# The last sequence's values in one half chunk, and the sample's output projection and MLP among the prompt's last MLP chunk

## The reference, cut to what matters

```python
def layer_out(x, attn, pool, mods, w_out, norm_mlp, w_up, w_down):
    _, _, g1, sh2, sc2, g2 = mods
    x = x + g1 * (jnp.concatenate([attn, pool], axis=-1) @ w_out)      # w_out 1024 x 1024
    h = rms_norm(x, norm_mlp) * (1 + sc2) + sh2
    return x + g2 * (jnp.square(jax.nn.relu(h @ w_up)) @ w_down)       # 1024 x 4096, 4096 x 1024

def reference(...):
    # prompt
    attn = moba_prompt(q, k, v, rel_bias)
    xp = layer_out(xp, attn, pool, mods, w_out, norm_mlp, w_up, w_down)
    # sample: scores over all past blocks, the best 3 blocks and the own one are weighed
    attn = moba_sample(q, k, v, cache_k, cache_v, l, page_table, rel_bias)
    xs = layer_out(xs, attn, pool, mods, w_out, norm_mlp, w_up, w_down)
    return rms_norm(xp, norm_final), rms_norm(xs, norm_final), ...
```

## Time and profile before

| what | us |
|---|---|
| timed runs | 897.68 median (897.31 to 902.81, 3 runs) |
| profiled launch | 903.88 |
| its span, first to last instruction | 902.0 |
| TensorE busy in the span | 841.3 (93%), 7634 matmuls |
| VectorE, ScalarE, GpSimd busy | 441.7, 338.1, 293.3 |
| mean granted TensorE clock | 0.976 |
| moved by DMA | 254.02 MB, mean 282 GB/s |

### The profile page before, as it was taken

The page is one execution under the profiler, slowest core; times in us unless marked ns, Lnnn a source line. Parts: engine busy times, 40 slices in busy tenths (PEclk is TensorE's granted clock), DMA queues, the critical chain, the costliest instruction groups (busy, mean ns, idle before and its releaser), DMA issues.

```text
span 902.0 us, 20195 instructions
## 1 busy us (share of the span) xinstructions
PE 841.3 (93%) x7634; PEld 592.8 (66%) x7634; DVE 441.7 (49%) x845; ACT 338.1 (37%) x701; POOL 293.3 (33%) x191
## 2 busy tenths in 40 slices
PE   5899999998999699999999999999999999999664
PEld 4577776666766266666666666666766666677553
DVE  2643222774776965575574564565564332013211
ACT  4133223886124646145145145154154254331110
POOL 0330003956221634244243343343333344440000
PEclk9699999999999699999999999999999999999988
DMA  9942236694999879999999999999999797779995
GB/s 294 326 153 94 94 106 256 194 343 147 323 299 308 284 260 333 303 310 333 304 301 341 300 322 322 298 314 329 301 318 373 247 333 257 235 251 349 399 397 213
DMA packets 167825, 254.02 MB, mean 282 GB/s; under 512 B 10454, under 2 KB 69419, under 8 KB 167755
## 3 DMA queue, kind: packets, MB, share of 16 engines
q1 hardware_dynamic: 166995, 250.66, 81.9%
q0 software_dynamic: 768, 2.51, 0.7%
HBM read 248.56 MB, written 4.75 MB: 281 GB/s over the span
## 4 chain that ended last, share of the span: by engine, by line
PE 82%; DVE 6%; DMA 3%; issue 3%; ACT 3%; SPq 3%; POOL 0%; DVEq 0%; ACTq 0%
PE PS L1523 78%; DMA W<-in_cache_v_dram 2%; SPq L501 2%; DMA mixT<-in_x_prompt_dram 1%; DVE W L1308 1%; DVE xT L1376 1%; PE PS L1872 1%; PE PS L1746 1%; PE PS L2055 1%; DVE mixT L1248 1%; DVE hT L1087 1%; SPq L496 1%; ACT mixT L878 1%; DVE mixT L1245 0%; DVE stat L1250 0%
## 5 line engine op out<-in xcount | busy, mean ns | idle before, releaser
L691 POOL TENSOR_TENSOR W_split<-W,W_split 128x1024 fp32r<-128x1024 f32 x72 | 172.8, 2399 | 289.0 <-ACT W_split L851 133.9
L1523 PE MATMUL PS<-gT_split,W_split 128*128 128x512 f32 x576 | 197.9, 404 | 1.2 <-DVE xT L1376 0.5
L1308 DVE STREAM_TRANSPOSE W<-rwT 128x512 f32<-128x512 f32 x256 | 162.7, 682 | 39.1 <-PE PS L1523 30.5
L1523 PE MATMUL PS<-rwT_split,W_split 128*128 128x512 f32 x512 | 174.9, 405 | 0.0
L1523 PE MATMUL PS<-hT_split,W_split 128*128 128x512 f32 x416 | 162.0, 399 | 0.5 <-ACT mixT L924 0.5
L1523 PEld LDWEIGHTS PS<-gT_split,W_split 128*128 128x128 f32 x576 | 108.1, 188 | 50.5 <-issue 14.8
L1523 PEld LDWEIGHTS PS<-rwT_split,W_split 128*128 128x128 f32 x512 | 97.1, 190 | 34.3 <-issue 14.8
L1523 PE MATMUL PS<-kT_split,W_split 128*128 128x512 f32 x256 | 100.0, 391 | 0.0
L851 ACT ACTIVATE W_split<-W 128x1024 fp32r<-128x1024 f32 x32 | 33.9, 1059 | 168.9 <-DMA W<-in_w_up_dram 168.8
L1376 DVE SCALAR_TENSOR_TENSOR xT<-PS,mods,xT 128x512 f32<-128x512 f32 x64 | 47.3, 742 | 97.0 <-PE PS L1523 96.8
L1523 PEld LDWEIGHTS PS<-hT_split,W_split 128*128 128x128 f32 x416 | 79.3, 191 | 16.7 <-issue 1.6
(11 more groups left out here) (276 smaller groups left out, 966.5 us busy)
## 6 DMA issues: line engine op xcount, KB each, us to landing
rwT<-in_cache_k_dram SPq DMA_DIRECT2D x256, 256.0 KB, 4.2
W<-in_cache_v_dram SPq DMA_DIRECT2D x256, 256.0 KB, 3.9
W<-in_w_ada_dram SPq DMA_DIRECT2D x12, 2048.0 KB, 10.8
W<-in_w_up_dram SPq DMA_DIRECT2D x32, 512.0 KB, 5.6
W<-in_w_down_dram SPq DMA_DIRECT2D x32, 512.0 KB, 5.5
W<-in_w_down_dram SPq DMA_DIRECT2D x5, 2048.0 KB, 17.3
W<-in_w_in_dram SPq DMA_DIRECT2D x3, 2048.0 KB, 7.9
rwT<-in_w_up_dram SPq DMA_DIRECT2D x3, 2048.0 KB, 11.4
```

The source lines that it names most:

```text
L691: pool.tensor_tensor(rows_part(RAW, q, W_split), rows_part(RAW, q), rows_part(HIGH, q, W_split), ALU.subtract).then_inc(w_low, 1)
L1308: dve.transpose(ktb[u % 2][:, :, g, :], k_ring[:, j % SLOTS, pg, :]).then_inc(kt_ev, 1)
L1523: return pe.matmul(out, lhsT, rhs, start=start, stop=stop, **kw)
```

## The change

The last sequence's values are weighed in `down(LAST - 1, ...)` alone, one unit after each tile. `turn_heads(LAST)`, the output projection, its fold, the mean square and the sample's MLP step 0 go among the matmuls of `up(LAST, ...)`; steps 1 to 4 go among those of `down(LAST, ...)`; steps 5 to 7 stay behind, now with the prompt's final rows (two blocks in step 5, one each in steps 6 and 7). The tail's slots are four instead of six, and SP's, ScalarE's and VectorE's lists follow the new order. Nothing is computed in another way.

```diff
-        tail_landed = [sem(f"tail_landed{i}") for i in range(6)]
+        tail_landed = [sem(f"tail_landed{i}") for i in range(4)]
...
-        tail_slots = [mixT[...], W[:, 0, :], rw[:, 0:4096], W[:, 1, :], hT[...], rw[:, 4096:8192]]
+        tail_slots = [mixT[...], W[:, 0, :], rw[:, 0:4096], W[:, 1, :]]
... SP
-            for u in range(UNITS):
-                section(LAST - 1, u, keys=False, values=u < UNITS - 1)
+            sp.wait_ge(up_ps, HP * LAST)
+            load_down(LAST - 1, 3)
+            for j in range(2, 4):
+                load_values(LAST, j)
+            for q in range(PARTS):
+                if q < PARTS - 1:
+                    for j in range(4 * q + 4, 4 * q + 8):
+                        load_values(LAST, j)
+                sp.wait_ge(dn_ps, FT * (LAST - 1) + 2 * q + 2)
+                load_up(LAST, q)
             sp.wait_ge(v_used, BLOCKS * DB)
             load_tail(3)
-            sp.wait_ge(up_ps, HP * DB)
-            load_down(LAST, 3)
+            sp.wait_ge(so_ps, 1)
             load_tail(4)
             load_tail(5)
-            sp.wait_ge(so_ps, 1)
+            sp.wait_ge(up_ps, HP * LAST + 1)
+            load_down(LAST, 0)
+            sp.wait_ge(up_ps, HP * LAST + 2)
+            load_down(LAST, 1)
+            sp.wait_ge(sup_ps, 1)
             load_tail(6)
+            sp.wait_ge(up_ps, HP * LAST + 3)
+            load_down(LAST, 2)
+            sp.wait_ge(sdn_ps, 1)
             load_tail(7)
+            sp.wait_ge(up_ps, HP * LAST + 4)
+            load_down(LAST, 3)
             for n in range(8, N_TAIL):
                 sp.wait_ge((sup_ps, sdn_ps)[n % 2], (n - TAIL_SLOTS) // 2)
                 load_tail(n)
... ScalarE, after front(LAST - 1); sample_relu(i) is the Relu of step i
+            up_high(LAST, 2)
+            up_high(LAST, 3)
+            hidden(LAST, 0)
+            act.wait_ge(so_ev, 1)
+            act.activation(hTs[:, :, :], xTs[:, :, :], ACT.Square).then_inc(sq_done, 1)
+            act.wait_ge(sms_ps, 1)
+            act.activation(rstds[:, :], bank(1, P, NS), ACT.Sqrt, ...).then_inc(root_done, 1)
+            hidden(LAST, 1)
+            down_high(LAST, 0)
+            sample_relu(0)
+            hidden(LAST, 2)
+            down_high(LAST, 1)
+            hidden(LAST, 3)
+            down_high(LAST, 2)
+            down_high(LAST, 3)
+            for i in range(1, N_CH):
+                sample_relu(i)
+                if i == 5:
+                    final_norm(0)
+                    final_norm(1)
+                elif i > 5:
+                    final_norm(i - 4)
             final_norm(TT)
... VectorE, in the loop over the steps; the rest of the sample's norm stands ahead of it
                 dve.wait_ge(sup_ps, i + 1)
                 dve.tensor_copy(up_sums, bank(0, P, P)).then_inc(sup_copied, 1)
+                if i == 1:
+                    ... square of step 1
+                    down_out(LAST, 0)
+                    down_out(LAST, 1)
+                    continue
+                if 2 <= i <= 4:
+                    down_out(LAST, 2 * i - 2)
                 ... square of step i
-                if 1 <= i <= TT:
-                    final_out(i - 1)
+                if 2 <= i <= 4:
+                    down_out(LAST, 2 * i - 1)
+                if i == 5:
+                    final_out(0)
+                    final_out(1)
+                elif i > 5:
+                    final_out(i - 4)
... TensorE, after back(LAST - 2)
+            down(LAST - 1, 0, 0, HP - 1)
+            turn_heads(LAST - 1)
+            down(LAST - 1, 1, 0, HP - 1)
+            weigh_values(LAST, 0)
+            down(LAST - 1, 0, HP - 1, HP)
+            weigh_values(LAST, 1)
+            down(LAST - 1, 1, HP - 1, HP)
+            for u in range(2, UNITS):
+                down(LAST - 1, u)
+                weigh_values(LAST, u)
+            up(LAST, 0, 0, 2)
+            turn_heads(LAST)
+            up(LAST, 0, 2, 4)
+            sample_out()
+            up(LAST, 0, 4, FT)
+            up(LAST, 1, 0, 4)
+            fold_out()
+            up(LAST, 1, 4, FT)
+            sample_mean_square()
+            up(LAST, 2, 0, 4)
+            sample_up(0)
+            up(LAST, 2, 4, FT)
+            fold_up(0)
+            up(LAST, 3, 0, 4)
+            sample_down(0)
+            up(LAST, 3, 4, FT)
+            sample_up(1)
+            down(LAST, 0, 0, HP - 1)
+            fold_up(1)
+            down(LAST, 1, 0, HP - 1)
+            sample_down(1)
+            down(LAST, 0, HP - 1, HP)
+            down(LAST, 1, HP - 1, HP)
+            for i in range(2, 5):
+                sample_up(i)
+                down(LAST, 2 * i - 2)
+                fold_up(i)
+                down(LAST, 2 * i - 1)
+                sample_down(i)
+            for i in range(5, N_CH):
+                sample_up(i)
+                fold_up(i)
+                if i == 5:
+                    final_rows(0)
+                    final_rows(1)
+                else:
+                    final_rows(i - 4)
+                sample_down(i)
```

More of the change, by code:

```diff
@@ L388, in block_landed @@
             return 16 * PPB * (ROUNDS * b + j // SLOTS + 1)
-        tail_slots = [mixT[:, :, :].rearrange("p a b -> p (a b)"), W[:, 0, :], rw[:, 0:4096], W[:, 1, :],
-                      hT[:, :, :].rearrange("p a b -> p (a b)"), rw[:, 4096:8192]]
+        tail_slots = [mixT[:, :, :].rearrange("p a b -> p (a b)"), W[:, 0, :], rw[:, 0:4096], W[:, 1, :]]
         TAIL_SLOTS = len(tail_slots)
@@ L1003, in _ @@
             front(LAST - 1)
[L1004 to L1011, removed]
             def final_norm(t):
@@ L1021, in final_norm, with sample_relu @@
                    .then_inc(fin_root, 1)
-            for i in range(N_CH):
+            def sample_relu(i):
                 act.wait_ge(sup_fold, i + 1)
@@ L1028, in _ @@
                    .then_inc(srelu, 1)
-                if 1 <= i <= TT:
-                    final_norm(i - 1)
+            up_high(LAST, 2)
[4 more added lines that the diff above has]
+            act.wait_ge(sms_ps, 1)
+            act.activation(rstds[:, :], bank(1, P, NS), ACT.Sqrt, bias=eps[:, 0:1], scale=1.0 / D).then_inc(root_done, 1)
+            hidden(LAST, 1)
[13 more added lines that the diff above has]
+                    final_norm(i - 4)
             final_norm(TT)
@@ L1471, in _ @@
             front(LAST - 1, keys=False, more=False)
-            back(LAST - 1, chain=False, more=False)
+            down_out(LAST - 1, FT - 1)
             own_heads(LAST)
             attention_sample(LAST)
-            down_out(LAST, 0)
-            down_out(LAST, 1)
             dve.wait_ge(so_ps, 1)
             dve.tensor_copy(folded, PS[:, 0:2, 0:P]).then_inc(so_copied, 1)
-            down_out(LAST, 2)
             dve.wait_ge(so_fold, 1)
@@ L1485, in _ @@
             dve.tensor_tensor(xTs[:, :, :], xTs[:, :, :], tmpS[:, :, :], ALU.add).then_inc(so_ev, 1)
-            down_out(LAST, 3)
             dve.wait_ge(so_ev, 1)
@@ L1490, in _ @@
             modulate_sample(1, SH2).then_inc(h2s_ready, 1)
-            for m in range(4, FT):
-                down_out(LAST, m)
             def final_out(t):
@@ L1506, in _ @@
                 dve.tensor_copy(up_sums, bank(0, P, P)).then_inc(sup_copied, 1)
+                if i == 1:
+                    dve.wait_ge(srelu, i + 1)
+                    dve.tensor_tensor(gS[:, i % 2, :, :], gS[:, i % 2, :, :], gS[:, i % 2, :, :], ALU.mult)\
+                       .then_inc(ssqr, 1)
+                    down_out(LAST, 0)
[3 more added lines that the diff above has]
+                    down_out(LAST, 2 * i - 2)
                 dve.wait_ge(srelu, i + 1)
@@ L2020, in piece_landed, with sample_out @@
+            weigh_values(LAST, 1)
[3 more added lines that the diff above has]
+                weigh_values(LAST, u)
             def piece_landed(n):
                 pe.wait_ge(*tail_lands(n))
-            pe.wait_ge(at_s, DB)
-            for c in range(D // PIECE):
-                piece_landed(c)
+            def sample_out():
+                pe.wait_ge(at_s, DB)
+                for c in range(D // PIECE):
+                    piece_landed(c)
+                    for k in range(FT):
+                        for g in range(QUADS):
+                            last = quarter(c, g, mixS[:, k, :], tail_slot(c)[:, k, g * P:(g + 1) * P],
+                                           k == 0, k == FT - 1, P)
+                last.then_inc(so_ps, 1)
@@ new lines, in fold_out, with sample_mean_square @@
+            def fold_out():
+                pe.wait_ge(so_copied, 1)
+                for c in range(D // PIECE):
+                    last = pe.transpose(bank(2, P, P, c * P), folded[:, c, :], ident)
+                last.then_inc(so_fold, 1)
+            def sample_mean_square():
+                pe.wait_ge(sq_done, TT + 1 + FT + 1)
+                for f in range(FT):
+                    last = mm(bank(1, P, NS), ones[:, :], hTs[:, f, :], f == 0, f == FT - 1)
```

(22 more changed lines are left out.)

1 line of the change is left out of this document (removed).

## The result

The changed kernel takes 893.68 us (median of 9 runs, 890.1 to 896.14). The kernel before, run beside it, takes 901.76 us (9 runs, 897.31 to 908.07). The ratio of the two is 0.9919 with a 95% interval of 0.9895 to 0.9943, 0.8% faster; the medians lie 8.1 us apart. That is clear of no change, but under the 1% from which the prediction would have called it faster (888.7 us). Forecast were 881 us and a range of 874 to 892, so the result lies outside. Of the miss of 12.7 us, 4.1 are the base: the forecast was hung on a median of three runs, 897.68, and the larger set has 901.76. Hung on that one, the range would have held the result, but not the gain: spans went from 902.0 to 894.3, 7.7 us shorter, where 16.5 were forecast, and that is the part to explain.

A forecast was written before the change was run, and what follows sets the result against it. Some 20 us of TensorE idle time in the sample's MLP tail, from step chains and instruction blocks through a full DMA, bounded it. Stages ending at 778.7, 812.1, 850.0, 871.1 led to 885.5, 16.5 saved: 881 us on the median, range 874 to 892.

The forecast's parts named there:

- the values' half: Down of chunk 6 with eight value units: 777.7 us plus 1.0 for late value loads, stage end 778.7.
- One new wait: Last down: sample down 1 waits 1.7 us (0 to 4), as ScalarE copies the last quarter before step 1's Relu.
- What would show it: The prediction's list of signs, including value waits of 0 to 3 us and stops 128 matmuls apart at the end.
- just hidden: Last weights in at 870 us, before sample down 7 wants them at about 873.4.
- rival A: Last three sample steps: instruction fetch is covered and the weights set the end; 877 us, chance 0.2.
- The weights' sum: From 786.1 us, 31.5 MB at 396 GB/s take 79.4, plus 2.5 and some 2 of gaps: in at 870.
- the last three steps: After the last down, three blocks of 256 TensorE instructions take 7.2, 7.2 and 6.5 us: from 850.0 to 871.1.
- The value units: Down of chunk 6: value loads turn around in 5.9 of 6.7 us; lateness 1.0 us, bounds 0 and 3.9.
- The final chain: After sample down 7, at the end of the kernel: 8.6 us, unchanged.
- The 0.7 us for the last copy: At the end, the prompt's last norm and write stand on VectorE ahead of the last copy, making it 0.7 late.
- B: Rival: blocks take 8.65 us each, values come 3.9 late, sample down 1 waits 4; 895.7, or 891; chance 0.2.
- C: Rival: the value ring turns too slowly, deciding from a turnaround of 15 us on; 906 us, chance 0.05.

The follow-up runs named there:

- e_square: Changed kernel with the square of sample step 1 on ScalarE behind its Relu instead of on VectorE; 890.94 us, ratio 0.9846 to the kernel before.
- e_order: Changed kernel with ScalarE's Relu of sample step 1 moved ahead of the last down quarter's high copy; 887.96 us, ratio 0.9835 to the kernel before.
- e_six: Changed kernel with six weight slots instead of four from piece 8 on, engine order kept; 893.25 us, ratio 0.9879 to the kernel before.
- e_order_six: Changed kernel with the edits of e_order and e_six together; 887.32 us, ratio 0.9812 to the kernel before.
- b_half: Kernel before, loading only half the bytes of the sample's MLP pieces 6 to 17, all matmuls kept; one profiled run, 892.17 us.
- order_half: e_order with only half the bytes of weight pieces 8 to 17 loaded, all instructions kept; one profiled run, 886.71 us.

## Why the prediction was off

Set beside the forecast, stage by stage: the values' half ends at 780.0 (forecast 778.7, +1.3); the last `up` takes 34.2 us (33.4, +0.8); the last `down` 43.9 (37.9, +6.0); from there to the end 36.2 (35.5, +0.7). These sum to 8.8, which is 16.5 less 7.7.

**The step that failed is "One new wait"**, in the last `down` with sample steps: forecast 1.7 us within 0 and 4, with the mechanism and the place right (a square on VectorE behind ScalarE, as named under "What would show it"). The cost was 4.88 us of waiting and some 2.6 us of slower work behind it. Three sizes were off.
- The quarter took 7.41 us to land and not 6.3. Piece 7, four times as large, had been issued 2.9 us ahead of it; that this is the reason was not tried by itself. 1.1 us.
- The square was taken at its usual length, 0.6 with the Relu. It took 2.37, since GpSimd's low part of the same quarter is released by the same copy. 2.1 us, and the wait in e_square is shorter by just these. It happens at two more places: an addition at 793.94, which took 2.53 us, and a square at 807.06, which took 1.22. This could be read before the change: the trace of the kernel before has it too, as in the fence below, where a VectorE instruction that takes 0.42 us at 390.86 takes 2.50. The Trainium skill (SBUF — State Buffer, section "SBUF: two separate sides") says that a VectorE instruction with two operands in SBUF and a GpSimd instruction share a pair of ports under an exclusive lock, held for a whole instruction. The traces agree: the square took 2.37 instead of 0.28 us, ending 0.15 us after GpSimd does.
- TensorE's granted clock. After the idle 4.9 us it is 0.56 on average over 6 us of work. Sample down 1 takes 3.64 us instead of 1.95, and the matmuls behind it the rest of the 2.6. The prediction costed such a stretch only for sample down 7 (1.0), and there it measured 3.59 instead of 1.95, 1.6.

VectorE and GpSimd in the kernel before:

```profile
723.53 2.50 DVE L1343 TENSOR_TENSOR cmps<-gate 128x256 f32<-128x256 f32 x1
...
723.18 2.58 POOL L691 TENSOR_TENSOR W_split<-W,W_split 128x1024 fp32r<-128x1024 f32 x1
```

**What follows from the wait was not costed at all.** "Behind that waiting matmul stands all of TensorE" was said, but not that SyncE stands behind it too: the next piece waits for sample down 1. The weights were forecast to be in at 870, "just hidden"; they are in at 881.92. Sample up 7 waits for a DMA of weights, which is the prediction's own sign for rival A: the weights set the end. e_order shows how much of it is the hole: with the wait gone they land 6.3 us earlier, and the stretch is 6.0 us shorter, 143.9 us where the forecast comes to 141.0.

**The weights' sum was short by itself.** In e_order, without the hole, they still land 131.2 us after the stretch's start, where the forecast of 870 makes 125.5, and sample up 7 still waits. The sum has some 2 us for gaps while a slot is awaited. By the windows of e_order, 28.1 us at 299 instead of 397 GB/s are worth some 6.9 us (an estimate from these two rows): the gaps lie in the last `up`, one of them where piece 6 waits for its slot. More slots at that place were not tried; those of e_six and e_order_six begin with piece 8, behind it, and no gain from them is shown.

**Right for the wrong reason: the last three steps.** They were forecast as three instruction blocks of 7.2, 7.2 and 6.5 us; the stretch came out within 0.7 us of that. But only one stop of 1.46 us is in it; the waits of 3.37 and 1.57 us for weights fill the place. The blocks are real (b_half, order_half), and they are the next limit, not this one.

**Right.** The value units lose 2.2 us in four of them (0.75, 0.89, 0.23, 0.34 above 1.06), within the bounds of 0 and 3.9. The last `up` with the output projection and step 0 came out as the sum of its instructions, but for 0.8 us before the mean square (the addition that GpSimd held up). Chains cost nothing between half chunks: from 831.5 to 858.0 TensorE is busy 26.50 of 26.50 us. The final chain took 8.7 us (forecast 8.6). The 0.7 us for the last copy behind the prompt's final rows is not paid here, where the weights come late; in e_order TensorE waits 1.50 us behind that copy instead of 0.56.

Of the rivals, A named what sets the end, but had the weights in at 870. B gave 6.3 us of gain in the span, near the 7.7 measured, but by other means: blocks of 8.65 (not there), values late by 3.9 (2.2), and a wait of 4 (4.88). C is refuted by the value units.

One reading was too wide: that the idle time lies in the stretch from 829.2 to 893.4 "and nowhere else". The earlier trace rows has TensorE busy 1.49 of the last 8.60 us too, and the change leaves that stretch as it was.

## What to carry to other kernels

When steps of a second chain are woven into a stream, look on every engine for what each link of the chain now stands behind, and move the link ahead of work that waits for a DMA; one move in ScalarE's order was worth 6 us here, nearly as much as the whole change. Then ask what runs on GpSimd beside each VectorE instruction of the chain, and which loads are issued only when a matmul of the chain is through: here 7.5 us of waiting and slow work on TensorE held back the loads too, so little of it could be caught up behind it.

## What the runs showed of the hardware

- A VectorE instruction of 0.28 us took 2.37 beside one of GpSimd of 2.34; on ScalarE the same square took 0.31 beside one of 2.37. In the kernel before, one of 0.42 took 2.50 beside one of 2.58.
- TensorE's stops between blocks of 256 instructions depend on the DMA's load: a block took 8.6 us at a DMA share of 0.96 and 6.2 to 6.5 at half the bytes. The block of 6.2 us ran beside a share of 0.20, so there is more to it than the load; what, the runs don't say.
- The granted clock after idle time: 0.56 on average (825.5 to 831.5) behind 4.9 us of idle time; 1.00 behind 2.79 us in e_square. The length of the gap alone does not settle it: before the mean square, e_order has a gap of 0.78 us with a clock of 0.72 on average over the 6 us from 794.2 on, and the changed kernel has the same gap and 1.00 behind it. What decides this stays open.
